# A decoder trunk's first 80 microseconds: loads and copies of the prologue put in another order

## The chip, the cores and the metric

One core of a Trainium2 chip. The time is the device time of one execution in microseconds (us); smaller is better. The profile is of one execution, the times are of several.

## The reference

Two layers (DEPTH = 2) of a decoder trunk for two groups of tokens with the same weights: a prompt of 512 tokens and 8 decode sequences of 4 tokens (32 tokens), width 1024.

```
sh1, sc1, g1, sh2, sc2, g2 = adaln(c, wm, bm)     # silu(c) @ w_mod + b_mod, 6 x 1024 columns
xn = rmsnorm(x, n1) * (1 + sc1) + sh1
a_q, a_kc, ... , m_if = split(xn @ wi, points)    # 2852 columns
x = x + g1 * (concat([a_out, m_out]) @ wo)        # sparse attention beside an mLSTM
xn2 = rmsnorm(x, n2) * (1 + sc2) + sh2
x = x + g2 * conv_ffn(xn2, ...)                   # up, causal conv, silu, gate, down
```

Everything is float32. Only what stands ahead of the first `xn @ wi` is touched here: the loads of x, of the conditions c (one row for the prompt, eight for decode) and of a block of constants, the first four of the twelve column parts of `silu(c) @ w_mod` (sh1 and sc1), and the sums of squares of the first rmsnorm.

## The kernel before, in words

The whole program is written by hand as five instruction streams (SyncE `sp`, TensorE `pe`, ScalarE `act`, VectorE `dve`, GpSimd `pool`), which meet only in semaphores. The tokens are kept turned: `xT` holds, for each of 8 chunks k of 128 features, 544 tokens in the free dimension. Ahead of the layers the prologue does this:

- SyncE issues loads of w_mod, 2 MB each (`load_mod`, L520 to L529): parts 0, 1 and 2 into the three slabs at once, part 3 into slab 1 when part 1 has been used (its turned result counts in `mod_t`). Then it waits for `load_in` (L530) and goes on to layer 0: slab pieces of w_in (`load_in_slab`, L551), each for L = 0 held back at L565 until a count of `mod_t` says that the slab is free; later the pages of the cache.
- GpSimd issues on its own queue the constants (1.6 MB), x_prompt (2 MB), x_sample, c_prompt, c_sample and the page table (L2281 to L2286), all counted in `load_in`, then nine small row loads (`rows_in`, L2294) and three more (L2301).
- ScalarE takes silu of the nine condition rows (L1260). TensorE waits for all six loads and for silu (L645, L646), turns the conditions (L648), then x: for each k four transposes of 128x128 and one of 32x128 (L655, L656) into one of three pairs of PSUM banks.
- For each k ScalarE copies the prompt's part from PSUM to `xT` (L1292), VectorE the decode part (L1618), and ScalarE squares the 544 tokens into one of two buffers `sq` (L1265, in `square`). TensorE adds the squares up over the partitions (`norm_sum`, L629: four calls), one chunk behind the transposes.
- VectorE and ScalarE make 1/rms of it (`inverse_root`, `root`), TensorE spreads it over the partitions (L640, L641) and turns the small rows (L683 to L685). Then for g = 0 to 3 `mod_part` (L669: 32 calls, which the trace shows as 64 matmuls) waits for its weights, ScalarE copies the result out (L1301), `mod_turn` turns it (L678) and VectorE adds the bias (L1667).
- After part 3 ScalarE splits the first w_in piece into a high part (L1308) and GpSimd makes the low part (`low_first`, L2309); VectorE, ScalarE and GpSimd make the scaled and shifted inputs in high and low parts (L1631, L1279, L1638, L2319 to L2323), and TensorE begins the input projection (L778).

Of the kernel before, what the change touches and what calls it, by code (L numbers as in the profile page):

```python
# [14 lines left out]
SEQ = 512  # L15
# [17 lines left out]
KC = D // 128  # L33
TS = NB * NT
TT = SEQ + TS
# [87 lines left out]
_WIDTHS = [a.shape[1] for a in shape_constants()][:len(_NAMES)]  # L123


def trunk_program(nc, A, O):
# [10 lines left out]
    with ctx:  # L137
# [203 lines left out]

        PRO_LOADS = 16 * 6
        pro_silu, pro_ct = ctx.enter_context(nc.semaphore("c_silu")), ctx.enter_context(nc.semaphore("c_transposed"))
        pro_xt = ctx.enter_context(nc.semaphore("x_transposed"))
        pro_copy_p, pro_copy_s = ctx.enter_context(nc.semaphore("x_copied_prompt")), ctx.enter_context(nc.semaphore("x_copied_decode"))
        load_in = ctx.enter_context(nc.semaphore("prologue_loaded"))
        final_tr, final_copy = sig("final_transposed", 10), sig("final_copied", 10)
# [21 lines left out]

        MODS = [(s, 0, c) for s, c in zip((0, 1, 2, 1), range(4))]  # L370
        MOD_FIRST = []
# [5 lines left out]
        MOD_FIRST.append(len(MODS))  # L377
        mod_in = [ctx.enter_context(nc.semaphore(f"mod_weights{s}_loaded")) for s in range(NSLAB)]
        mod_acc, mod_copy, mod_t, mod_add = (sig("mod_accumulated", len(MODS)), sig("mod_part_copied", len(MODS)),
# [132 lines left out]
        def _(sp):  # L512
# [7 lines left out]
            def load_mod(g):  # L520

                s, L, c = MODS[g]
                sp.dma_start(slab[s][:, :].rearrange("p (k n) -> p k n", k=8),
                             wmod[L, :, :, 512 * c:512 * c + 512]).then_inc(mod_in[s], 16)

            for g in range(4):
                if g == 3:
                    sp.wait_ge(mod_t.sem, mod_t.at(2))
                load_mod(g)  # L529
            sp.wait_ge(load_in, PRO_LOADS)  # L530
            flat = lambda a: a.rearrange("l n p a k d -> (l n) p (a k d)")
            cmp_pool, sel_pool = flat(A["cache_cmp_kv"]), flat(A["cache_sel_kv"])

            for L in range(DEPTH):
# [26 lines left out]
                for i in range(4):  # L561
                    if i in (0, 1, 3):
                        load("in", (0, 1, 1, 2)[i], [])
                    if L == 0 and i in (0, 1, 3):
                        sp.wait_ge(mod_t.sem, mod_t.at((1, 4, 4, 3)[i]))  # L565
                    load_in_slab(i)
# [52 lines left out]
        def _(pe):  # L619
# [23 lines left out]
            for s in range(NSLAB):  # L643
                pe.sem_inc(slab_out[s], 1)
            pe.wait_ge(load_in, PRO_LOADS)  # L645
            pe.wait_ge(pro_silu, 1)  # L646
            for k in range(KC):
                ins = tr(ps[7][:, 9 * k:9 * k + 9], crow[0:9, 128 * k:128 * k + 128], idn(9))  # L648
            ins.then_inc(pro_ct, 1)
            for k in range(KC):  # L650
                if k >= 3:
                    pe.wait_ge(pro_copy_p, k - 2)
                    pe.wait_ge(pro_copy_s, k - 2)
                for t in range(PT_):
                    tr(ps[2 * (k % 3)][:, 128 * t:128 * t + 128], xrow[:, t, 128 * k:128 * k + 128], ident)  # L655
                tr(ps[2 * (k % 3) + 1][:, 0:TS], crow2[0:TS, 128 * k:128 * k + 128], idn(TS)).then_inc(pro_xt, 1)  # L656
                if k:
                    norm_sum(0, k - 1)
            norm_sum(0, KC - 1)
            spread(0)  # L660

            def mod_part(g, bank):

                s, _, _ = MODS[g]
                pe.wait_ge(*mod_loads(g))
                wv = slab[s][:, :].rearrange("p (k n) -> p k n", k=8)
                for k in range(KC):
# [11 lines left out]

            pe.wait_ge(pro_copy_p, KC)  # L680
            pe.wait_ge(pro_copy_s, KC)
            pe.wait_ge(rows_in, ROWS)
# [573 lines left out]
        def _(act):  # L1256
            A_ = nc.scalar.activation
            drain = act.drain
            act.wait_ge(load_in, PRO_LOADS)
            A_(crow[0:9, :], crow[0:9, :], ACT.Silu).then_inc(pro_silu, 1)  # L1260
# [29 lines left out]
            for k in range(KC):  # L1290
                act.wait_ge(pro_xt, k + 1)
                A_(xT[:, k, 0:SEQ], ps[2 * (k % 3)][:, :], ACT.Copy).then_inc(pro_copy_p, 1)  # L1292
                act.wait_ge(pro_copy_s, k + 1)
                drain()
                square(0, k)
# [310 lines left out]
        def _(dve):  # L1606
# [9 lines left out]
            for k in range(KC):  # L1616
                dve.wait_ge(pro_xt, k + 1)
                cp(xT[:, k, SEQ:TT], ps[2 * (k % 3) + 1][:, 0:TS]).then_inc(pro_copy_s, 1)  # L1618

# [659 lines left out]
        def _(pool):  # L2279
            ld = pool.dma_start  # L2280
            pool.dma_start(cst[:, :], A["shape_constants"][:, 0:sum(_WIDTHS)]).then_inc(load_in, 16)  # L2281
            ld(xrow[:, :, :], A["x_prompt"][0].rearrange("(t p) d -> p t d", p=128)).then_inc(load_in, 16)
            ld(crow2[0:TS, :], A["x_sample"].rearrange("b t d -> (b t) d")).then_inc(load_in, 16)
            ld(crow[0:1, :], A["c_prompt"]).then_inc(load_in, 16)
            ld(crow[1:9, :], A["c_sample"]).then_inc(load_in, 16)
            ld(pages_sb[:, :], A["page_table"].rearrange("b n -> (b n)").unsqueeze(0)).then_inc(load_in, 16)  # L2286
            r8 = lambda a: a.rearrange("l (k n) -> (l k) n", n=128)
# [179 lines left out]
```

## Time and profile before

| | |
|---|---|
| times of three runs | 1967.26, 1955.88, 1967.9 us (median 1967.26) |
| the profiled execution | 1970.02 us, of it a span of 1968.2 us |
| TensorE busy | 1742.1 us, 89% of the span |
| VectorE, ScalarE, GpSimd busy | 919.3, 617.9, 206.2 us |
| mean granted TensorE clock | 0.919 of full speed |
| DMA | 218.82 MB, mean 111 GB/s |

An engine's busy time says how much work it has; where the time of the whole comes from is read from what TensorE waits for in each stretch.

### The profile page before, as it was taken

Reading aid. Unit: us, or ns where it says so; the run is one execution under the profiler, and the core shown is the slowest. Engines: PE = TensorE matmul, PEld = TensorE weight load, DVE = VectorE, ACT = ScalarE, POOL = GpSimd, SP = SyncE. Lnnn points to the kernel's source line nnn. Section 1 sums busy time; section 2 is a strip of 40 time slices with the busy share of each in tenths; the row PEclk is TensorE's granted clock in tenths of the full one; section 3 lists DMA queues with packets and bytes.
Section 4 is the critical chain, followed back from the end, with each engine's and each line's share of the span. In section 5 each row is a group of like instructions: output and inputs, shape, how many; then the busy total and the mean of one; then the engine's idle time right before and its main releaser. Section 6 shows DMA issues by size and latency. Waiting matters only on the chain.

```text
span 1968.2 us, 37164 instructions
## 1 busy us (share of the span) xinstructions
PE 1742.1 (89%) x14719; PEld 1544.3 (78%) x14719; DVE 919.3 (47%) x2318; ACT 617.9 (31%) x1173; POOL 206.2 (10%) x317
## 2 busy tenths in 40 slices
PE   4699997977879999999979998788768999999996
PEld 3599865545779999999969986534558899999995
DVE  0433434534545555555453343453452645545643
ACT  2232133532324224223232223353231523323313
POOL 2101002432100000000010100133310000000001
PEclk9799978978889999999979998787879999999998
DMA  6435385348522222221123528410772122222201
GB/s 217 132 97 175 87 299 180 111 126 233 106 74 87 86 83 87 85 85 43 46 79 93 182 92 303 122 33 24 220 148 86 44 86 85 85 85 85 85 22 50
DMA packets 154282, 218.82 MB, mean 111 GB/s; under 512 B 11722, under 2 KB 112394, under 8 KB 153964
## 3 DMA queue, kind: packets, MB, share of 16 engines
q1 hardware_dynamic: 145152, 193.23, 31.1%
q0 software_dynamic: 9008, 23.94, 4.4%
q8 instruction: 80, 1.31, 0.3%
q14 instruction: 42, 0.34, 0.1%
HBM read 200.45 MB, written 16.68 MB: 110 GB/s over the span
## 4 chain that ended last, share of the span: by engine, by line
PE 77%; issue 6%; DVE 5%; ACT 3%; DMA 2%; POOL 2%; SPq 2%; DVEq 1%; POOLq 0%; ACTq 0%
PE ps L1177 27%; PE ps L1203 14%; PE ps L778 13%; PE ps L1156 4%; PE ps L868 3%; PE ps L880 2%; PE ps L895 2%; DMA slab<-in_w_up 2%; PE ps L669 2%; PE ps L821 1%; POOL xnT L2371 1%; PE ps L771 1%; PE ps L770 1%; DVE xnT L1631 1%; SPq L538 1%
## 5 line engine op out<-in xcount | busy, mean ns | idle before, releaser
L1177 PE MATMUL ps<-work_r,big_r 128*128 128x272 f32 x1408 | 294.3, 290 | 19.8 <-DVE xnT_r L1656 13.4
L1177 PE MATMUL ps<-work_r,slab_r 128*128 128x272 f32 x1408 | 292.6, 289 | 0.0
L1177 PE MATMUL ps<-xnT_r,big_r 128*128 128x272 f32 x1408 | 290.6, 288 | 0.0
L1177 PEld LDWEIGHTS ps<-work_r,big_r 128*128 128x128 f32 x1408 | 221.4, 189 | 22.8 <-issue 21.5
L778 PE MATMUL ps<-slab_r,work_r 128*128 128x256 f32 (+1 forms) x1024 | 228.6, 287 | 0.0
L1177 PEld LDWEIGHTS ps<-xnT_r,big_r 128*128 128x128 f32 x1408 | 222.8, 189 | 0.0
L1177 PEld LDWEIGHTS ps<-work_r,slab_r 128*128 128x128 f32 x1408 | 221.5, 189 | 0.0
L1656 DVE TENSOR_TENSOR slab_r<-slab,big_r 128x2048 fp32r<-128x2048 f32 (+2 forms) x72 | 168.9, 2349 | 62.0 <-ACT big_r L1536 54.2
L778 PEld LDWEIGHTS ps<-slab_r,work_r 128*128 128x128 f32 x1024 | 174.2, 193 | 2.7 <-issue 2.5
L1203 PE MATMUL ps<-side_r,big_r 128*128 128x272 f32 x704 | 148.3, 292 | 4.9 <-DVE big_r L1656 4.9
L1554 ACT ACTIVATE big<-big,work 128x560 f32<-128x560 f32 x44 | 33.7, 766 | 369.9 <-DVE big L2212 369.9
L1203 PE MATMUL ps<-big_r 128*128 128x272 f32 x704 | 146.2, 289 | 0.0
L1203 PE MATMUL ps<-side_r,slab_r 128*128 128x272 f32 x704 | 145.9, 289 | 0.0
L2160 DVE TENSOR_TENSOR work<-ps,modT 128x32 f32<-128x32 f32 x112 | 21.5, 192 | 254.4 <-PE ps L1203 184.4
L778 PE MATMUL ps<-work_r 128*128 128x256 f32 (+1 forms) x384 | 115.8, 302 | 17.1 <-DVE xnT_r L1638 17.1
L2332 POOL DMA_DIRECT2D out<-work x32 | 18.3, 575 | 1067.2 <-ACT work L1592 822.2
L1203 PEld LDWEIGHTS ps<-side_r,big_r 128*128 128x128 f32 x704 | 111.1, 190 | 7.7 <-DVE big_r L1656 5.4
L1203 PEld LDWEIGHTS ps<-big_r 128*128 128x128 f32 x704 | 111.5, 190 | 0.0
L778 PE MATMUL ps<-work_r,xnT_r 128*128 128x256 f32 (+1 forms) x384 | 111.4, 290 | 0.0
L1203 PEld LDWEIGHTS ps<-side_r,slab_r 128*128 128x128 f32 x704 | 111.1, 190 | 0.0
L1536 ACT ACTIVATE big_r<-slab 128x2048 fp32r<-128x2048 f32 x44 | 84.4, 1918 | 68.4 <-PE ps L1177 55.8
L778 PEld LDWEIGHTS ps<-work_r 128*128 128x128 f32 x384 | 74.8, 195 | 25.3 <-DVE xnT_r L1638 11.5
(432 smaller groups left out, 3129.1 us busy)
## 6 DMA issues: line engine op xcount, KB each, us to landing
slab<-in_w_mod SPq DMA_DIRECT2D x24, 2048.0 KB, 9.2
slab<-in_w_up SPq DMA_DIRECT2D x44, 1024.0 KB, 7.5
slab<-in_w_in SPq DMA_DIRECT2D x20, 1024.0 KB, 5.5
slab<-in_w_down SPq DMA_DIRECT2D x20, 1024.0 KB, 5.8
slab<-in_cache_cmp_kv SPq DMA_DIRECT2D x128, 128.0 KB, 2.0
slab<-in_cache_sel_kv SPq DMA_DIRECT2D x96, 128.0 KB, 2.0
big<-in_cache_win_kv SPq DMA_DIRECT2D x16, 512.0 KB, 5.3
out<-big POOLq DMA_DIRECT2D x16, 448.0 KB
```

The source lines that it names most:

```text
L669: ins = mm(bank[32 * q:32 * q + 32, 0:128], cT[:, k, :], wv[:, k, 128 * q:128 * q + 128], start=k == 0, stop=k == KC - 1, tile_position=(0 ...
L778: ins = mm(ps[n % 4][:, 0:cw], x, fr(wt[:, k, :]), start=k == 0 and m == 0, stop=k == KC - 1 and m == 2)
L868: mm(ps[2 * (s % 2) + k][:, 0:nk], qT[h_, g, 128 * t:128 * t + 128], (ksT, kwT)[br][h_, 0:nk], start=True, stop=True).then_inc(a_s.sem, 1)
L880: ins = tr(ps[4 + k][:, 128 * i:128 * i + 128], Pq[:, u % 4, 128 * i:128 * i + 128], ident)
L895: ins = mm(ps[6][64 * k:64 * k + 64, 128 * i:SEQ], proj[:, i, c + 64 * k:c + 64 * k + 64], PT[:, n % 2, k, 512 * i:384 * i + SEQ], start=b ...
L1156: ins = mm(ps[2 * (c % 3) + b][:, 0:HALF], wt, fr(x[:, k, HALF * b:HALF * b + HALF]), start=k == 0 and n == 0, stop=k == KC - 1 and n == 2)
L1177: ins = mm(ps[2 * half + b][:, 0:HALF], wt, fr(x[:, k, HALF * b:HALF * b + HALF]), start=k == 0 and n == 0, stop=k == KC - 1 and n == 2)
L1203: ins = mm(ps[bank + b][:, 0:HALF], wt, fr(x[:, k, HALF * b:HALF * b + HALF]), start=k == 0 and n == 0, stop=k == n_k - 1 and n == 2)
L1536: A_(fr(hiU[:, q % 2, :, :, :]), src[:, :, :, cc:cc + 128], ACT.Copy).then_inc(w_hi.sem, 1)
L1554: A_(cv[:, s, 0:UPW - 2], cv[:, s, 0:UPW - 2], ACT.Silu, bias=cbias[:, s:s + 1]).then_inc(u_si.sem, 1)
L1656: return tt(fr(dst), dst, fr(hi).bitcast(F), ALU.subtract)
L2160: tt(tmp.rearrange("p (b t) -> p b t", b=NB), hi[:, SEQ - HALF:HALF].rearrange("p (b t) -> p b t", b=NB), bc(gs, 2, NT), ALU.mult)
```

## The change

Five edits, all in the prologue:

1. The constants, x_prompt and x_sample are issued by SyncE on its own queue, ahead of the w_mod parts. They count in semaphores of their own (`k_in`, `x_in`); the conditions and the page table stay on GpSimd's queue and count in `c_in`.
2. w_mod part 3 gets a place of its own, in the unused columns 4096 to 8191 of `big`, so that its load waits for nothing. The pieces of w_in for slab 1 wait for a lower count.
3. TensorE waits for the constants, then silu, turns the conditions, and only then waits for x.
4. VectorE copies both parts of each turned chunk from PSUM to `xT`; ScalarE only squares. One semaphore `pro_copy` takes the place of two, and ScalarE's `drain` is gone.
5. `norm_sum` runs two chunks behind the transposes instead of one.

```diff
-        MODS = [(s, 0, c) for s, c in zip((0, 1, 2, 1), range(4))]
+        MODS = [(s, 0, c) for s, c in zip((0, 1, 2, 3), range(4))]
...
+        mod_at = [t[:, :] for t in slab] + [big[:, 4096:8192]]
...
+            sp.dma_start(cst[:, :], A["shape_constants"][:, 0:sum(_WIDTHS)]).then_inc(k_in, 16)
+            sp.dma_start(xrow[:, :, :], A["x_prompt"][0].rearrange("(t p) d -> p t d", p=128)).then_inc(x_in, 16)
+            sp.dma_start(crow2[0:TS, :], A["x_sample"].rearrange("b t d -> (b t) d")).then_inc(x_in, 16)
             for g in range(4):
-                if g == 3:
-                    sp.wait_ge(mod_t.sem, mod_t.at(2))
                 load_mod(g)
-            sp.wait_ge(load_in, PRO_LOADS)
+            sp.wait_ge(c_in, 48)
...
-                        sp.wait_ge(mod_t.sem, mod_t.at((1, 4, 4, 3)[i]))
+                        sp.wait_ge(mod_t.sem, mod_t.at((1, 2, 2, 3)[i]))
...
-            pe.wait_ge(load_in, PRO_LOADS)
+            pe.wait_ge(k_in, 16)
             pe.wait_ge(pro_silu, 1)
             for k in range(KC):
                 ins = tr(ps[7][:, 9 * k:9 * k + 9], crow[0:9, 128 * k:128 * k + 128], idn(9))
             ins.then_inc(pro_ct, 1)
+            pe.wait_ge(x_in, 32)
             for k in range(KC):
                 if k >= 3:
-                    pe.wait_ge(pro_copy_p, k - 2)
-                    pe.wait_ge(pro_copy_s, k - 2)
+                    pe.wait_ge(pro_copy, k - 2)
...
-                if k:
-                    norm_sum(0, k - 1)
+                if k >= 2:
+                    norm_sum(0, k - 2)
+            norm_sum(0, KC - 2)
             norm_sum(0, KC - 1)
...
-            act.wait_ge(load_in, PRO_LOADS)
+            act.wait_ge(c_in, 48)
...
-                act.wait_ge(pro_xt, k + 1)
-                A_(xT[:, k, 0:SEQ], ps[2 * (k % 3)][:, :], ACT.Copy).then_inc(pro_copy_p, 1)
-                act.wait_ge(pro_copy_s, k + 1)
-                drain()
+                act.wait_ge(pro_copy, k + 1)
                 square(0, k)
...
                 dve.wait_ge(pro_xt, k + 1)
-                cp(xT[:, k, SEQ:TT], ps[2 * (k % 3) + 1][:, 0:TS]).then_inc(pro_copy_s, 1)
+                cp(xT[:, k, 0:SEQ], ps[2 * (k % 3)][:, :])
+                cp(xT[:, k, SEQ:TT], ps[2 * (k % 3) + 1][:, 0:TS]).then_inc(pro_copy, 1)
...
-            pool.dma_start(cst[:, :], A["shape_constants"][:, 0:sum(_WIDTHS)]).then_inc(load_in, 16)
-            ld(xrow[:, :, :], A["x_prompt"][0].rearrange("(t p) d -> p t d", p=128)).then_inc(load_in, 16)
-            ld(crow2[0:TS, :], A["x_sample"].rearrange("b t d -> (b t) d")).then_inc(load_in, 16)
-            ld(crow[0:1, :], A["c_prompt"]).then_inc(load_in, 16)
-            ld(crow[1:9, :], A["c_sample"]).then_inc(load_in, 16)
-            ld(pages_sb[:, :], A["page_table"].rearrange("b n -> (b n)").unsqueeze(0)).then_inc(load_in, 16)
+            ld(crow[0:1, :], A["c_prompt"]).then_inc(c_in, 16)
+            ld(crow[1:9, :], A["c_sample"]).then_inc(c_in, 16)
+            ld(pages_sb[:, :], A["page_table"].rearrange("b n -> (b n)").unsqueeze(0)).then_inc(c_in, 16)
```

## Rows read from the trace of the kernel before

**Rows 1.** Windows: stretch, length, each engine's busy us, granted clock, DMA share, GB/s
```profile
0.00:82.00 82.00, 37.92 (x403) 26.74 (x403) 19.57 (x40) 22.61 (x35) 17.45 (x26) 0.86 0.61 209
82.00:300.00 218.00, 211.99 (x1930) 189.18 (x1929) 79.83 (x196) 58.27 (x124) 17.47 (x23) 0.94 0.48 154
```
**Rows 2.** Timeline of TensorE and ScalarE, 21 to 40 us
```profile
21.12 1.05 ACT L1260 ACTIVATE work<-work 9x1024 f32<-9x1024 f32 x1 [19.08 <-DMA pages_sb<-in_page_table]
...
23.24 1.11 PE L655 MATMUL ps<-shape_constants,work 128*128 128x128 f32 x4
...
26.63 1.12 PE L655 MATMUL ps<-shape_constants,work 128*128 128x128 f32 x4
...
36.13 1.12 PE L655 MATMUL ps<-shape_constants,work 128*128 128x128 f32 x4
...
37.52 0.60 ACT L1292 ACTIVATE xT<-ps 128x512 f32<-128x512 f32 x1 [0.56 <-PE ps L656]
38.20 0.66 ACT L1265 ACTIVATE big<-xT 128x544 f32<-128x544 f32 x1
...
38.91 0.68 PE L629 MATMUL ps<-big,shape_constants 128*32 128x136 f32 x8 [0.81 <-ACT big L1265]
```
**Rows 3.** Timeline, 44 to 72 us: from the first mod part to the input projection
```profile
44.50 3.64 PE L669 MATMUL ps<-slab,cT 128*32 128x128 f32 x64
...
48.80 1.95 PE L669 MATMUL ps<-slab,cT 128*32 128x128 f32 x64
...
52.00 14.31 SPq L558 DMA_DIRECT2D slab<-in_w_in  x5
...
59.69 3.64 PE L669 MATMUL ps<-slab,cT 128*32 128x128 f32 x64 [5.59 <-DMA slab<-in_w_mod]
...
63.57 2.11 ACT L1308 ACTIVATE work_r<-slab 128x2304 fp32r<-128x2304 f32 x1
...
65.77 5.03 POOL L2309 TENSOR_TENSOR slab_r<-slab,work_r 128x2304 fp32r<-128x2304 f32 x1 [54.68 <-ACT work_r L1308]
...
71.50 0.58 PE L778 MATMUL ps<-work_r 128*128 128x288 f32 x1 [7.30 <-DVE xnT_r L1638]
```
**Rows 4.** DMA issues, 0 to 150 us: count, KB each, median us to landing
```profile
slab<-in_w_in SPq DMA_DIRECT2D x5, 1024.0 KB, 5.3
...
work<-in_x_prompt POOLq DMA_DIRECT2D x1, 2048.0 KB, 17.3
...
pages_sb<-in_page_table POOLq DMA_DIRECT2D x1, 0.2 KB, 16.8
```
**Rows 5.** DMA issues, 0.7 to 1.2 us: w_mod part 0
```profile
slab<-in_w_mod SPq DMA_DIRECT2D x1, 2048.0 KB, 14.7
```
**Rows 6.** Windows of the first 35 us: the last column is GB/s moved
```profile
5.00:10.00 5.00, 0.00 (x0) 0.00 (x0) 0.00 (x0) 0.00 (x0) 5.00 (x11) 1.00 1.04 433
10.00:15.00 5.00, 0.00 (x0) 0.00 (x0) 0.00 (x0) 0.00 (x0) 1.08 (x2) 1.00 1.01 395
...
30.00:35.00 5.00, 5.00 (x38) 2.92 (x33) 0.50 (x3) 3.63 (x6) 0.00 (x0) 1.00 0.11 41
```
**Rows 7.** GpSimd's small loads later: DMA issues of 290 to 480 us
```profile
side<-in_state_mlstm_n POOLq DMA_DIRECT2D x2, 8.0 KB, 5.5
```
**Rows 8.** Source line L2417, GpSimd's load of the conv history
```profile
DMA to landing us min/median/max: 11.7/15.0/18.3
```
**Rows 9.** Groups of VectorE copies from PSUM: busy us, mean ns, idle before
```profile
L1992 DVE COPY work<-ps 128x512 f32<-128x512 f32 x24 | 16.6, 691 | 22.3 <-PE ps L991 22.1
...
L1618 DVE COPY xT<-ps 128x32 f32<-128x32 f32 x8 | 1.5, 191 | 12.6 <-PE ps L656 12.6
```
**Rows 10.** Timeline of SyncE's queue: the issue of w_mod part 2
```profile
1.89 10.11 SPq L523 DMA_DIRECT2D slab<-in_w_mod  x1
```
**Rows 11.** Windows from part 3 on: the figure before DMA share is the clock
```profile
60.00:65.00 5.00, 3.80 (x65) 2.84 (x57) 0.58 (x3) 1.61 (x2) 0.00 (x0) 0.50 0.48 132
...
85.00:100.00 15.00, 15.00 (x117) 14.81 (x116) 4.74 (x11) 3.79 (x7) 0.00 (x0) 0.97 0.04 11
```

## Blind prediction of the change's time

> **What bounds the kernel now.** I read the windows first. In the first 82 us TensorE is busy for 37.92 us, and from 82 to 300 us for 211.99 of 218 [rows 1]. The reader is to see two things there: the change lies wholly in a stretch where TensorE mostly waits, and right behind it TensorE is full, so what the prologue saves moves everything behind it forward and nothing behind it takes it back by waiting for a transfer. The gain can't be larger than a part of the 44 us that TensorE doesn't work in these 82. Then I read the timeline, for what ends each wait.
>
> - Until 21 us nothing runs. ScalarE's silu starts at 21.12, released by the load of the page table, the last of the six [rows 2]; that load needed 16.8 us, and x_prompt 17.3 [rows 4], while SyncE's queue carried w_mod parts nobody needed until 44.50 [rows 3]. DMA moved 433 and 395 GB/s from 5 to 15 us [rows 6]: the transfers are not slow, they share, and the needed bytes come with unneeded ones.
> - From 23.24 to the last norm sum, which starts at 38.91, the turned chunks set the pace: one each (36.13 - 26.63) / 5 = 1.90 us [rows 2], with TensorE busy for 5.00 of 5 us from 30 to 35 [rows 6].
> - From 44.50 the four mod parts run. Part 3 starts only at 59.69, after 5.59 us of waiting for its weights [rows 3].
> - From there a fixed chain leads to the projection: ScalarE's split at 63.57, GpSimd's low part at 65.77, TensorE's first product at 71.50 [rows 3].
>
> **Part 1, the load order.** SyncE's queue now carries constants (1630.5 KB), x_prompt (2048 KB) and x_sample (128 KB) first, 3.90 MB. A 1024 KB load alone needs 5.3 us from issue to landing [rows 4]; at 395 GB/s its bytes take 2.65, so 2.65 us are start and completion. That queue begins at about 0.8 us (part 0's issue in the window of [rows 5]), so x is there at 0.8 + 2.65 + 3.90 / 0.395 = 13.3 us. GpSimd's small loads (some 0.46 MB with the 256 KB gains) share the engines; if all come ahead of x they add 1.2 us. I take half: 13.8, and TensorE starts with x at 13.9 in place of 23.24, **9.3 us** earlier. Bounds: 12.5 us (at the 433 GB/s of [rows 6], nothing shared) and 15 us, so 10.7 to 8.2. That SyncE's queue serves its loads one after the other is seen in w_mod part 0: landed 14.7 us after its issue [rows 5], with two more parts behind it and half of the rate going to GpSimd's queue.
>
> This holds only if silu and the turned conditions are ready by 13.9. From the landing of the last condition load to the first transpose of x it was 23.24 - 21.07 = 2.2 us (silu's start at 21.12 less 0.05 of waking [rows 2]), so the cover ends if `c_in` fills later than 11.7. GpSimd issues the three at 1.3 to 2.8 us. The nearest row for a small load on its queue while SyncE's is full is 8 KB in 5.5 us [rows 7], which gives 8.3; the far row is the conv history, 16 rows of 11 KB, with 11.7 to 18.3 us [rows 8], which gives 14 to 21. I take the nearer row, since the three loads are 36 KB together, and keep the other as a rival. The nine small row loads are needed first at about 34 us; even as late as in the far row they are there.
>
> Of the queues passed: GpSimd's sheds three issues, some 2 us that nobody waited for. SyncE's gets three loads ahead of the w_mod parts. One issue there can hold the queue for 10.11 us when two parts are ahead of it [rows 10]; with four parts it may be held until about 30 us, and SyncE's next duty, the first w_in piece, falls due at 39. The weights: the queues ran dry in the slice from 30 us on, in which they moved 41 GB/s [rows 6], so at 30.5; 2.1 MB more are moved now (part 3 comes in the same burst), so part 3 lands at 30.5 + 5.3 + 1 = 37, and part 0 at 13.8 + 5.3 = 19, where it is needed at 34.6. Every part is early.
>
> **Part 2, norm sums two behind and copies on VectorE.** The pace of 1.90 us is TensorE's own work, and its instructions stay the same, so the pace stays. What goes is the wait for the first square: chunk 2 began 3.39 us after chunk 0 [rows 2]; without a sum between them it begins after 2 x 1.28 = 2.56 (1.28 is the pace of 1.90 less 0.62 for a sum, which [rows 2] bound by its 0.68 from first start to last end), and chunk 7 at 4.46 + 4 x 1.90 = 12.06 after chunk 0 in place of 12.89. Against that stands the last chunk's tail, which is serial: VectorE's copy takes 0.69 us [rows 9] where ScalarE's took 0.60 [rows 2], and the decode copy of 0.19 [rows 9] now runs behind it instead of beside it; some of it overlaps, so the tail grows by 0.2 us (0.1 to 0.3). The cover of the copies elsewhere is large: 0.88 us of VectorE and 0.66 of ScalarE in a pace of 1.90. Sum: 0.83 - 0.2 = **0.6 us**, 0.3 to 0.8. With both edits the last sum starts at 13.9 + 15.05 = 29.0 in place of 38.91: 9.9 us.
>
> **Part 3, a place for mod part 3.** Nothing between 38.91 and 44.50 is changed, so part 0 starts at 34.6. Parts follow at 1.95 + 0.66 = 2.61 us (48.80 less the end of part 0 at 48.14, plus the length of part 1) [rows 3], so in the profile of before part 3 could have begun at 48.80 + 2 x 2.61 = 54.02. It began at 59.69: 5.67 us. It also took 3.64 us where part 1 took 1.95 [rows 3]; the granted clock from 60 to 65 us is 0.50, the 1.2 GHz level [rows 11], and TensorE had been idle before it. Directly behind part 2 it runs like part 1: 1.69 us, and 0.15 in its turn. Sum **7.5 us**; if the clock falls or rises otherwise, 5.7 to 7.5. (Part 0 took 3.64 us as well, beside a granted 1.00 in the windows: its duration, not that column, says that it ran at the lower level. It may run so again; if it should find the clock up, 1.7 us more are won, and if part 1 is still at the lower level, 1.7 lost.)
>
> **Part 4, the first w_in piece.** It used to be issued at 52.00 [rows 3]. Its own wait (`mod_t` 1, part 0 turned) was met when part 1 began, at about 48.9, and SyncE hung on part 3's slab. Now it is issued at 48.9 - 9.9 = 39.0 and lands some 6 us later (5.3 for 1024 KB [rows 4], it has 1152), at 45.2. ScalarE wants it at 63.57 - 17.4 = 46.2. So it is just hidden, by 1.0 us; what it comes later than that costs as much again. I take nothing, bound 1 us lost. The other pieces of w_in come 20 us earlier, which is worth nothing: behind 82 us TensorE didn't wait for them [rows 1]. Split, low part, shift and scale (63.57 to 71.50) are untouched and just move.
>
> **Sum.** 9.3 + 0.6 + 7.5 = 17.4 us. The profiled execution of 1970.02 us becomes 1952.6; against the median of 1967.26 that is 1949.9. **Forecast 1950.** The bounds of the terms together give a gain of 13.2 to 20.7 us, or 1946.6 to 1954. A measurement here tells about 1%, 19.7 us, from no change, and the forecast stands just inside it: a real gain that is nearly all of 1%.
>
> **Rival A: the conditions come late (1956).** x is early, but silu waits for three small loads on GpSimd's queue. If they come like the conv history, at 14 to 21 us, take 17.5 [rows 8], TensorE starts x at 19.7, and the first term shrinks from 9.3 to 3.5: gain 11.6, 1955.7. Against it speak [rows 7], and the old order itself: x_prompt, issued at 2.0, landed at 19.3, and the page table, three loads on, at 21.1 [rows 2, 4], 0.6 us for each small one beside a full SyncE queue. For it: the pieces now ahead are long rows (12.7 KB of constants, 4 KB of x), and a small load may have to let whole runs of them pass. The Trainium skill, "DMA: Bandwidth & Descriptors", section "Queues, rings and completion order", says that each DMA engine goes round the queues that have work in whole packets, some 9 to 17 descriptors and up to 64. By that rule a condition load could wait for an engine's share of the constants and the next for one of x, which would put this rival's time in the forecast's place; the trace of before has only short pieces in SyncE's queue and can't show it.
>
> **Rival B: slower, the small loads come last (1974).** The same place, taken to its end: what is on GpSimd's queue lands only when SyncE's has run dry, at about 36.3 us now. Then x starts at 38.5, 15.3 us later than before; less 0.6 and 7.5 that makes 7.2 us lost, 1974.5. It decides from `c_in` at 21.07 + 8.1 = 29.2 us on. Against it: on GpSimd's queue the page table landed at 21.1 us, 9 us before SyncE's, just as full, ran dry [rows 2, 6].
>
> **Rival C: the gain is there at 82 us and the clock moves the rest (1943 or 1957).** The three runs of before lie 12 us apart with the same program, more than most terms here, and the clock falls and rises at places that depend on when TensorE pauses: after the mod parts it stood at 0.50, and only from 85 us on at 0.97 [rows 11]. The new pause, between part 3 and the first product, is about 8 us, as the old second one was, so I expect the same fall. If the clock should stay up, 1.6 us are won at the start of the projection, and later phases may turn out either way by some 6 us.
>
> **How the numbers follow.** The forecast's mechanism 0.70; A 0.14; B 0.03; C 0.13. With the spread of the runs (12 us between three) laid over the forecast, about four in ten of its share, and half of C's, end beyond 19.7 us: 0.35 faster by over 1%. Slower by over 1% needs B and more: 0.02. The rest, 0.63, is within 1%. Range 1940 to 1960: above it takes in A and a forecast that falls on a slow run, below a forecast that falls on a run like the 1955.88.
>
> **What would show it.** Right: the page (or the conditions) releases silu before 10 us; the first transpose of x waits for x_prompt and starts at 13 to 15; the last norm sum is 15.0 to 15.2 us behind it; the fourth mod part starts 0.7 us behind the third and takes 1.95 us; GpSimd's low part starts at 47 to 50; the first product at 52.5 to 56, 16 to 19 us earlier than 71.50; from there the same work in the same time. Wrong: silu released after 11.7 (A) or 29 us (B); a wait of ScalarE for the w_in piece; a fourth mod part of 3.64 us; a stretch behind the prologue that is longer by more than a microsecond or two at another granted clock (C).

## The result, and the profile after

The changed kernel takes 1949.28 us (median of 13 runs, 1945.96 to 1956.36), the kernel before 1961.3 us (13 runs, 1950.9 to 1967.9). The ratio is 0.9946 with an interval of 0.9926 to 0.9966: faster by 10.6 us, 6.7 to 14.5, clearly different from nothing and within 1%. The forecast said 1950, by a gain of 17.4 us against a median of three runs that lay 6 us too high; the time was met, the gain was three fifths of what was forecast. Three single executions further down (of 2009, 2042 and 2832 us, one in each of three versions) ran at a granted clock of 0.56 to 0.83 where the others have 0.92, and count in no ratio.

The timeline of the changed kernel from the load of the conditions to the first input product, against [rows 2, 3]:

```profile
8.27 1.06 ACT L1262 ACTIVATE work<-work 9x1024 f32<-9x1024 f32 x1 [6.23 <-DMA pages_sb<-in_page_table]
...
17.52 1.12 PE L657 MATMUL ps<-shape_constants,work 128*128 128x128 f32 x4 [7.05 <-DMA work<-in_x_sample]
...
32.52 0.68 PE L631 MATMUL ps<-big,shape_constants 128*32 128x136 f32 x8 [0.50 <-ACT big L1267]
...
38.10 2.78 PE L672 MATMUL ps<-slab,cT 128*32 128x128 f32 x64
...
41.72 7.03 SPq L560 DMA_DIRECT2D slab<-in_w_in  x5
...
46.77 1.96 PE L672 MATMUL ps<-big,cT 128*32 128x128 f32 x64
...
48.97 2.11 ACT L1307 ACTIVATE work_r<-slab 128x2304 fp32r<-128x2304 f32 x1
...
51.16 5.03 POOL L2306 TENSOR_TENSOR slab_r<-slab,work_r 128x2304 fp32r<-128x2304 f32 x1 [41.90 <-ACT work_r L1307]
...
56.90 0.58 PE L780 MATMUL ps<-work_r 128*128 128x288 f32 x1 [7.45 <-DVE xnT_r L1638]
```

Read it as a chain of differences. Silu starts 12.9 us earlier, but x's first transpose only 5.7 (17.52 for 23.24), and TensorE waited 7.05 us for it: silu is no longer what is late, x is. The last norm sum is 6.4 us earlier, part 0 too, part 3 12.9 us (46.77 for 59.69), the first product **14.6 us** (56.90 for 71.50). The loads in the first 60 us of that trace, against [rows 4], with the columns as there:

```profile
work<-in_x_prompt SPq DMA_DIRECT2D x1, 2048.0 KB, 14.6
...
shape_constants<-in_shape_constants SPq DMA_DIRECT2D x1, 1630.5 KB, 6.9
...
work<-in_x_sample SPq DMA_DIRECT2D x1, 128.0 KB, 15.8
...
pages_sb<-in_page_table POOLq DMA_DIRECT2D x1, 0.2 KB, 5.8
```

and its windows, the last column GB/s, against [rows 6]:

```profile
5.00:10.00 5.00, 0.53 (x5) 0.56 (x6) 0.00 (x0) 1.06 (x1) 4.26 (x8) 1.00 1.00 351
10.00:15.00 5.00, 0.47 (x5) 0.37 (x4) 0.23 (x1) 0.00 (x0) 0.00 (x0) 1.00 0.98 296
```

The DMA engines are as busy as before (shares 1.00 and 0.98) and move 351 and 296 GB/s where they moved 433 and 395. The constants are in at 7.7 us, x_prompt at 15.8, x_sample, 128 KB behind it, only at 17.5.

In all the two profiled executions are 24 us apart (1970.02 and 1945.99), which is 9 more than the prologue gives. The profiled run of before was slower than all 13 timed ones. With the matmuls of the two traces matched one by one, the lead of the changed kernel is 14.6 us at the first product, 15.2 at 300 us of the kernel before, 11.8 at 330, 7.3 at 600, 9.6 at 1060, 6.1 at 1200 and 22.4 at 1600. So it loses 3.4 us from 300 to 330 and 4.5 more up to 600, and what it wins late is mostly a wait that one execution of before had in layer 1. Both are taken up below.

### The profile page after: what moved, and what is told of

It is laid out like the page before. It is cut to its first block, busy times and chain, and to the rows that moved or that the text cites. A ratio compares the mean times of both kernels' runs of the same rounds, so it can differ in the third digit from the quotient of the medians.

```text
span 1944.2 us, 37157 instructions
## 1 busy us (share of the span) xinstructions
PE 1733.2 (89%) x14719; PEld 1540.3 (79%) x14719; DVE 924.1 (48%) x2326; ACT 613.2 (32%) x1165; POOL 203.6 (10%) x314
## 4 chain that ended last, share of the span: by engine, by line
PE 78%; issue 5%; DVE 5%; ACT 3%; DMA 2%; POOL 2%; SPq 2%; DVEq 1%; POOLq 0%; ACTq 0%
PE ps L1179 27%; PE ps L1205 14%; PE ps L780 13%; PE ps L1158 4%; PE ps L870 2%; PE ps L897 2%; PE ps L882 2%; PE ps L672 2%; DMA slab<-in_w_up 2%; POOL xnT L2368 1%; PE ps L823 1%; PE ps L773 1%; PE ps L772 1%; SPq L540 1%; DVE xnT L1631 1%
## 5 line engine op out<-in xcount | busy, mean ns | idle before, releaser
L1179 PE MATMUL ps<-work_r,big_r 128*128 128x272 f32 x1408 | 295.0, 291 | 19.3 <-DVE xnT_r L1656 13.4
```

The lines of the kernel that those rows point to most:

```text
L1179: ins = mm(ps[2 * half + b][:, 0:HALF], wt, fr(x[:, k, HALF * b:HALF * b + HALF]), start=k == 0 and n == 0, stop=k == KC - 1 and n == 2)
```

## The experiments

In each, "x" is the start of the first transpose of x, "product" that of the first input product. Before: 23.24 and 71.50; changed: 17.52 and 56.90. These two come from one trace each; the unchanged parts of other traces show how far such a time repeats (the first run of the pair without state stores has the prologue of before, product at 71.27; the second that of the changed kernel, 57.33).

**Each part alone.**

The order alone:

```diff
...
+            sp.dma_start(cst[:, :], ...).then_inc(k_in, 16)      # then x_prompt, x_sample: x_in
             for g in range(4):
                 if g == 3:
                     sp.wait_ge(mod_t.sem, mod_t.at(2))
                 load_mod(g)
-            pe.wait_ge(load_in, PRO_LOADS)
+            pe.wait_ge(k_in, 16)
...
+            pe.wait_ge(x_in, 32)                                  # ahead of x's transposes
```

> The kernel before with the load order alone (constants, x_prompt, x_sample first on SyncE's queue, conditions and pages on GpSimd's); mod part 3 still waits for slab 1, copies and sums as before. Theory: the order alone makes x's first transpose start at 17.5 us as in the changed kernel (before: 23.24), 5.7 us earlier, and the whole chain up to the first input product moves by that: 71.5 - 5.7 = 65.8 us. Rival 1: the late landing of x comes from part 3 being in the same burst: then x starts here at 14 to 15 us. Rival 2: the wait for part 3's weights eats the gain (its load is issued by a fixed event, not earlier): first product at 71.

x at 17.36, product at 61.92, 1949.75 us in one run (before on that chip 1966.03). x came as the theory had it, so part 3 in the burst is not what makes x late. The product came 3.9 us earlier than expected. The timeline shows why:

```profile
20.75 1.12 PE L660 MATMUL ps<-shape_constants,work 128*128 128x128 f32 x4
...
24.26 0.66 PE L660 MATMUL ps<-shape_constants,work 128*128 128x128 f32 x4
...
30.63 0.68 PE L633 MATMUL ps<-big,shape_constants 128*32 128x136 f32 x8 [0.96 <-ACT big L1270]
...
36.22 2.51 PE L674 MATMUL ps<-slab,cT 128*32 128x128 f32 x64
...
50.12 3.64 PE L674 MATMUL ps<-slab,cT 128*32 128x128 f32 x64 [5.43 <-DMA slab<-in_w_mod]
```

Four transposes took 1.12 us at 20.75 and 0.66 at 24.26: by their duration the clock came up to its upper level in the middle of them (the granted clock reads 1.00 there, and in the kernel before too), which it did in neither the kernel before nor the changed one. From x to the last sum it was 13.3 us in place of 15.7, and part 0 took 2.51 for 3.64. 2.4 + 1.1 us of this gain are that, 5.9 the order, 0.2 a shorter wait for part 3, which was still 5.43 us.

Part 3's own place alone:

```diff
-        MODS = [(s, 0, c) for s, c in zip((0, 1, 2, 1), range(4))]
+        MODS = [(s, 0, c) for s, c in zip((0, 1, 2, 3), range(4))]
...
-                if g == 3:
-                    sp.wait_ge(mod_t.sem, mod_t.at(2))
...
```

> The kernel before with a place of its own for mod part 3 alone. Theory: x starts at 23.2 us as before, the fourth part starts 0.7 us behind the third and runs in 1.95 us, first input product at 71.5 - 7.5 = 64.0 us. Rival: four parts in the burst delay GpSimd's loads of constants and x, which share the engines: x at 25 us or later, product at 66 us or later.

x at 23.4, product at 61.92 (9.6 us earlier), 1949.13 us in one run. The rival falls: four parts in the burst delay GpSimd's loads by nothing that shows. Part 3 ran at 51.80 for 1.96 us, right behind part 2. Here too the clock came up in the transposes (part 0 at 42.76 for 44.50, and 3.16 us long): 2.2 of the 9.6 us. The place gives 7.4.

Copies and sums alone:

```diff
-                if k:
-                    norm_sum(0, k - 1)
+                if k >= 2:
+                    norm_sum(0, k - 2)
+            norm_sum(0, KC - 2)
             norm_sum(0, KC - 1)
...
-                A_(xT[:, k, 0:SEQ], ps[2 * (k % 3)][:, :], ACT.Copy).then_inc(pro_copy_p, 1)
+                cp(xT[:, k, 0:SEQ], ps[2 * (k % 3)][:, :])        # on VectorE
```

> The kernel before with the copies on VectorE and the sums two chunks behind alone. Theory: from the first transpose of x to the last norm sum 15.0 us in place of 15.67, first input product at 71.5 - 0.6 = 70.9 us, with part 3's wait moved by as much. Rival: VectorE's longer copies and ScalarE's wait for them take the gain back: 15.7 us, product at 71.5 us.

The last sum at 38.36, 15.00 us behind x for 15.67 and 0.55 us earlier than 38.91 (x came at 23.36); the product at 69.83, 1.7 us earlier, of which 0.7 are a part 0 of 2.91 us and 0.4 part 3's load, which needed a little less. 1958.32 us in one run. The term was right in the prologue, and this trace has something else, which comes below.

All but the order:

> The kernel before with part 3's own place, the copies on VectorE and the sums two behind, but the old load order. Theory: the parts add up: x starts at 23.2 us, first input product at 71.5 - 7.5 - 0.6 = 63.4 us (up to 2.5 less if the clock rises earlier), run time 6 to 10 us below the kernel before. On where the rest of the changed kernel's gain went: in three of three traces with the new load order and with the state stores, TensorE waited 5 to 7 us ahead of the second norm of layer 0 for a late w_up, in none of the three traces with the old order. If that belongs to the order, this kernel doesn't show it in layer 0 and its runs are no slower than those of the changed kernel by more than 3 us; if it is chance, it may show it and its runs are some 6 us slower than the changed kernel's. In the same way a stretch of layer 0 (303 to 342 us) took 3.4 us longer in the four traces with the copies' edit and in no other: if it belongs to the edit, it is here.

x at 23.16, product at 62.22 (expected 63.4, up to 2.5 less; part 0 took 2.47). 1955.78 us, ratio 0.9976 (0.9955 to 0.9997): 5 us faster, 1 to 9. The parts add up in the prologue. With the order on top the ratio is 0.9946 (0.9926 to 0.9966): the two intervals overlap, so that the order adds to the run time what it adds in the prologue (5.9 us by the ratios) is likely, but barely clear of nothing. Of the two readings that the expectation offered neither fits whole: TensorE waited only 1.7 us in layer 0, as if the lateness belonged to the order, and the runs are some 6 us slower than the changed kernel's, as if it were chance. The stretch of layer 0 took 40.8 us, halfway between the two lengths.

**What makes x late.** Four versions of the changed kernel. The three edits below make one version each; the fourth has the first and the third:

```diff
+            pool.wait_ge(x_in, 32)       # rows and gains later: here
             r8 = lambda a: a.rearrange("l (k n) -> (l k) n", n=128)
...
```

```diff
+            pool.wait_ge(x_in, 32)       # the gains alone later: here
             load_gains(0)
```

```diff
             sp.dma_start(crow2[0:TS, :], ...).then_inc(x_in, 16)
+            sp.wait_ge(x_in, 32)         # weights after x
             for g in range(4):
                 load_mod(g)
```

Rows and gains later:

> The changed kernel with GpSimd waiting for x before it issues its nine row loads and three loads of gains (0.42 MB). Theory (the small loads of GpSimd's queue slow x): x starts at 13.9 to 14.5 us in place of 17.52, and the first input product comes at 53 to 54 us in place of 56.9. Rival (the engines fall out of step by themselves, with the w_mod parts behind x in the same queue filling them): x starts at 16.5 to 17.5 us.

The gains alone later:

> The changed kernel with only the three gain loads (260 KB of the 0.46 MB) held back until x is there. Theory: DMA moved only 141 GB/s in a stretch at 13.5 to 15 us, where a 256-byte packet of the b_if gains took 862 ns on each of 16 engines; that stall and the 256 KB are most of the delay, x starts at 14.5 to 15.5 us. Rival: the nine row loads with their short rows are the delay, and x starts at 16 to 17.5 us.

The weights after x:

> The changed kernel with SyncE waiting for x before it issues the four w_mod parts; GpSimd's small loads as in the changed kernel. Theory (GpSimd's small loads slow x, not the w_mod parts behind it in the same queue): x starts at 16 to 17.5 us as in the changed kernel. Rival (DMA engines that are through with x go on with w_mod and take bandwidth from those that aren't): x starts at 14 to 15 us. The mod parts then land at about 17 + 2.6 + 21 = 40 us, part 0 at 25 us, before they are needed at 38 and 46 us.

Rows, gains and weights, all after x:

> The changed kernel with both: GpSimd's row and gain loads and SyncE's w_mod parts held back until x is there. Theory: with nothing beside or behind them the constants and x move at the full rate, x starts at 13.2 to 13.8 us against 14.0 with the small loads alone held back, and the first input product comes at 53.3 to 54 us; the mod parts land by 38 us and part 0 by 21 us, before they are needed. Run time 14 to 18 us below the kernel before. Rival: the gap between the end of x and the first w_mod bytes delays part 3 or the first w_in piece, and ScalarE's split starts later than 46 us.

| held back until x is there | x | product |
|---|---|---|
| nothing (changed kernel) | 17.52 | 56.90 |
| w_mod | 15.52 | 55.08 |
| gains | 15.22 | 54.69 |
| rows and gains | 13.93, 14.2 | 54.06, 53.46 |
| rows, gains, w_mod | 13.66 | 53.24 |

The timeline of the version with rows and gains later, and under it that with all three:

```profile
13.93 1.11 PE L657 MATMUL ps<-shape_constants,work 128*128 128x128 f32 x4 [3.74 <-DMA work<-in_x_sample]
```

```profile
13.66 1.12 PE L658 MATMUL ps<-shape_constants,work 128*128 128x128 f32 x4 [3.38 <-DMA work<-in_x_sample]
```

With GpSimd's twelve small loads out of the way x starts at 13.93 and 14.2. So 3.3 to 3.6 us of lateness go with 0.42 MB of small loads, for which their bytes account for 1.1 at 395 GB/s. But the loads are only half of it: w_mod held back with the small loads left in place gives 2.0 us too (15.52, between what theory and rival said), and once the small loads are gone w_mod costs just 0.3 to 0.5. Both rivals were partly right: the two work together. What fits all five rows is that the small loads put the DMA engines out of step, and an engine that is through with x goes on to w_mod while another still has x to move; no row here shows single engines, so this is argued, not shown. The gains' 260 KB cost 2.3 us, the rows' 160 KB 1.0 to 1.3. The slow packets named in the expectation go with the delay that small loads and w_mod make together: in the three traces that have the order with nothing held back, 15 or 16 packets of 256 bytes took 0.5 to 1.3 us each at about 13.5 us; with gains or w_mod held back none took over 0.03 us before x was there. From 13.5 to 14.0 us DMA moved 36 GB/s in the changed kernel, 180 with the gains held back and 285 with w_mod held back. Whether these packets cause the delay or share its cause is not shown.

The three single runs and the timed version that belong to this: 1944.09 (gains), 1947.99 (w_mod), 1958.84 (rows and gains); all three held back 1951.95 us, ratio 0.9943 (0.9920 to 0.9965). That is 11 us below the kernel before where 14 to 18 were expected, and no better than the changed kernel's 0.9946, though its product comes 3.7 us earlier. The version with rows and gains later was timed:

> The changed kernel with GpSimd's row and gain loads held back until x is there, timed. Theory: the prologue is 17.4 us shorter than before (first input product at 54.1 us, as in its trace), so the runs are about 3 us below the changed kernel's and 14 us (0.7%) below the kernel before's. Rival: the rows that come later make no difference in the run time, or the late w_up in both layers (5 to 6 us each in its first trace) belongs to the new order and costs what was won: 8 to 11 us below the kernel before.

1946.74 us, ratio 0.9914 (0.9885 to 0.9943): 16.8 us faster than before, 11 to 22, for an expected 14. The holding back of w_mod on top makes the prologue 0.2 to 0.8 us shorter and shows no gain in the runs.

**Where the rest went: the copies' edit again.** Rows and gains later, and the copies and sums as in the kernel before:

```diff
-                    pe.wait_ge(pro_copy, k - 2)
+                    pe.wait_ge(pro_copy_p, k - 2)
+                    pe.wait_ge(pro_copy_s, k - 2)
...
-                cp(xT[:, k, 0:SEQ], ps[2 * (k % 3)][:, :])
+                A_(xT[:, k, 0:SEQ], ps[2 * (k % 3)][:, :], ACT.Copy).then_inc(pro_copy_p, 1)   # on ScalarE
```

> The changed kernel with GpSimd's row and gain loads held back until x is there, and with the copies and sums as in the kernel before (ScalarE copies, sums one behind). Theory: x starts at 14.0 us, from there to the last norm sum 15.7 us in place of 15.0, first input product at 54.1 + 0.6 = 54.7 us. The stretch of layer 0 that took 39.1 us in the four traces without the copies' edit and 42.5 in the seven with it (partly so in one more) tells whether that edit causes it: 39.1 here if it does, and then the runs are 2 to 3 us below those of the version with the edit. Rival: that stretch depends on when the work starts against the clock's steps, and takes 42.5 us here too. The late w_up of layer 0 (5 of 6 traces with the new order and the state stores): about 5 us of waiting if it belongs to the order.

x at 14.2, product at 54.30. **1942.05 us, ratio 0.9879 (0.9849 to 0.9910)**: 23.7 us faster than before, 17.7 to 29.6, and the lowest ratio of all. The version that differs from it by the copies' edit alone is the one above, on another chip, with 0.9914: 0.35% or 7 us more, but the intervals overlap, so these two don't show by themselves that the edit costs time. On the same chip the one with the edit, w_mod held back too and a product 1.1 us earlier gave 1951.95 and 0.9943, and there the intervals don't touch; those 12.6 us are far more than the 3.2 that follow, and the rest isn't explained. The traces show the 3.2. The chain in time, in the stretch named (columns: start, us, what); first before, then the changed kernel, then the copies' edit alone, then this version:

```profile
314.99 4.24 PE ps L844 x24
319.23 0.79 PE ps L848 x8
320.02 1.03 PE ps L850 x8
...
322.17 4.72 PE ps L858 x32
```

```profile
300.02 5.38 PE ps L846 x24
305.41 1.18 PE ps L850 x8
306.59 1.03 PE ps L852 x8
...
308.74 6.35 PE ps L860 x32
```

```profile
312.98 5.38 PE ps L843 x24
318.36 1.17 PE ps L847 x8
...
321.68 6.36 PE ps L857 x32
```

```profile
297.21 4.24 PE ps L847 x24
301.45 0.79 PE ps L851 x8
...
304.39 4.71 PE ps L861 x32
```

The same instructions on the same data, 200 us behind the edit: 10.8 us in the first and the last, 13.9 in the two between. They are transposes, behind 8.5 us in which TensorE does one short transpose, and they start at the lower clock; in the one kind the clock comes up during the first 24, in the other one step later. The windows that hold them say so, granted clock 0.76 before and 0.63 after:

```profile
315.00:328.00 13.00, 11.87 (x80) 11.30 (x80) 4.09 (x10) 3.08 (x4) 1.78 (x3) 0.76 0.80 293
```

```profile
300.00:313.00 13.00, 11.85 (x64) 11.59 (x64) 3.15 (x7) 3.07 (x4) 1.76 (x3) 0.63 0.84 304
```

Of the traces with the edit 8 of 9 have the long form, of those without it none of 5 (the ninth is the one with the old order and part 3's place). When the work starts doesn't decide it: the start moved by 17 us between them in either group.

What links a copy at 20 us to the clock at 315 stands in the traces, on ScalarE. In the chain ahead of the transposes it squares eight 128x128 blocks, one after the other. In all nine traces with the edit, and in none of the five without, it stands idle for 0.34 us ahead of one of them, always the same instruction of its stream, and waits there for nothing that the profile shows ("issue"); TensorE's wait behind it is 4.19 us for 3.92. The changed kernel, and then TensorE's short transpose before and after:

```profile
290.52 0.31 ACT L1380 ACTIVATE work<-big 128x128 f32<-128x128 f32 x1 [0.34 <-issue]
```

```profile
310.37 0.30 PE L678 MATMUL ps<-shape_constants,aTs 128*128 128x128 f32 x1 [3.92 <-DVE modT L1667]
```

```profile
295.40 0.30 PE L681 MATMUL ps<-shape_constants,aTs 128*128 128x128 f32 x1 [4.19 <-DVE modT L1667]
```

The transposes so start 0.27 us later, counted from the last work of TensorE. In the five traces of the short form without the edit they start 3.9 us after the granted clock has fallen, and it rises 2.9 us after their start; in the eight of the long form they start 4.1 to 4.4 us after the fall, and it rises 5.8 to 6.1 us after their start. Before (fall at 311.08, start at 314.99), then after (fall at 295.86, start at 300.02), the clock being the figure before the DMA share:

```profile
311.10:317.80 6.70, 2.81 (x13) 2.81 (x14) 4.48 (x5) 0.60 (x1) 1.78 (x3) 0.50 0.83 246
318.00:324.70 6.70, 5.57 (x51) 5.31 (x49) 2.39 (x5) 2.33 (x3) 0.00 (x0) 1.00 1.04 378
```

```profile
295.90:306.00 10.10, 5.97 (x29) 5.98 (x29) 5.96 (x7) 2.58 (x4) 1.76 (x3) 0.50 0.93 273
306.20:309.40 3.20, 2.07 (x18) 1.81 (x18) 1.01 (x3) 0.29 (x1) 0.00 (x0) 1.00 1.05 380
```

In the ninth trace with the edit the pause is there, but the clock fell 6.7 us ahead of the transposes and rose 3.5 us behind their start: the short form. So the rival had a point too: in these traces the form goes with where the start stands between the clock's steps, and the edit moves it by 0.27 us. No run sets that pause by itself, so this last link is not shown by an experiment but read from 14 traces that agree, and why ScalarE pauses at that instruction is open. Not every such difference goes with the edit: from 1060 to 1200 us a stretch is 3.2 to 3.5 us longer in six of the nine traces with it and in two of the five without.

**Where the rest went: the late w_up.** In the profiled run of before TensorE waited 11.4 us ahead of the second norm of layer 1 (the waits of TensorE from 1440 to 1500 us), in the changed kernel 6.7 us at the same place of layer 0 (485 to 545 us). Before, then after:

```profile
PE ps L629 <- ACT big L1265: 11.4, 1, 11.4
```

```profile
PE ps L631 <- ACT big L1267: 6.7, 1, 6.7
```

The chain behind both leads to a 1 MB load of w_up, which landed a median of 34.6 us and 30.9 us after its issue, where the same load of layer 0 in the kernel before took 24.9. It shares the engines with GpSimd's stores of the decode groups' mLSTM states. So those were left out of both kernels:

```diff
...
                 for s_ in range(2):
                     for q_ in range(2):
                         pool.wait_ge(ms_Cc.sem, ms_Cc.at(3 * q_ + 3, L))
                         h = 2 * q_ + s_
-                        put(s_C[L][:, h].rearrange("b k v -> k b v"), ...)
-                        pool.dma_start(s_n[L][:, h].rearrange("b k -> k b"), ...)
```

> The kernel before without the stores of the decode groups' mLSTM states C and n (16 DMAs in two layers; those two outputs are left out). In the trace of before the load of w_up ahead of the second norm of layer 1 lands only 37.7 us after its issue, beside those stores, whose packets take up to 1 us each, and TensorE waits 11.4 us; in layer 0 1.2 us. Theory: without the stores w_up lands in time in both layers, the run time falls by 5 to 15 us and the spread of the runs shrinks from 17 us to under 6 us. Rival: the late landing has another cause (the load of the conv history, the order of the queue): no change in time and spread.

1952.24 us, ratio 0.9945 (0.9926 to 0.9963) against before, and runs from 1946.9 to 1956.9 where before has 1952.9 to 1970.3: 10.8 us faster with a spread of 10 us for 17. The DMA issues of that stretch of layer 0:

```profile
slab<-in_w_up SPq DMA_DIRECT2D x2, 1024.0 KB, 19.8
...
work<-in_state_ffn_conv POOLq DMA_DIRECT2D x1, 176.0 KB, 3.8
```

w_up lands after 19.8 us for 24.9, and the conv history, which needed 11.7 to 18.3 us [rows 8], after 3.8. The theory holds in its main point; the spread shrank less than it said.

> The changed kernel without the same stores (those two outputs are left out). Theory: the prologue's gain is 14.6 to 15.0 us in every run, and what hides part of it in the medians is the chance landing of w_up; with that taken away this kernel is 13 to 16 us faster than the kernel before without the stores. Rival: the moved start gives back some 4 us later in the kernel for a reason of its own: the two differ by 8 to 12 us here too.

1945.54 us, ratio 0.9911 (0.9884 to 0.9938) against before. By the ratios it is 0.34%, 6.7 us, below the same without the stores in the kernel before, and the two intervals allow 0 to 13. Expected were 13 to 16; the rival said 8 to 12 and lies inside those bounds. The theory that only chance hides the 14.6 us doesn't hold: of its missing part the copies' edit explains 3.2 us (this trace has the long form too), and some 4 us by the medians stay open.

Whether the late w_up belongs to the new order is not settled. In layer 0 TensorE waited 5.2 to 11.1 us in seven of eight traces with the order and the stores, and 1.1 to 1.7 in four of four with the old order. Yet the trace with 11.1 is of the best version, whose profiled run, 1950.2 us, was the slowest of its six, and that of before, with its 11.4 in layer 1, slower than its 13. A profile shows one draw; the runs say that the lateness comes and goes in both kernels.

## Why the forecast was right, and where it was off

- **Part 1, the load order: the term mis-sized.** Forecast 9.3 us, measured 5.7. The step that failed is "if all come ahead of x they add 1.2 us. I take half": small loads were charged by half of their bytes at the full rate, 0.6 us. They cost 3.3 to 3.6: 1.9 by themselves (15.52 for 13.66) and the rest only with w_mod behind x, for which the forecast has no term. The base under it, 2.65 us and 3.90 MB at 395 GB/s, gives a start at 13.4 with no small load in the way; held back they leave 13.9 to 14.2, and 13.66 with w_mod held back too, so it was right to within 0.3 to 0.8 us. The bound of 15 us was too near as well.
- The cover of silu held: the page table needed 5.8 us, for the 5.5 of [rows 7], and silu started at 8.27. Rival A is dead, and with it what the forecast made of the Trainium skill, "DMA: Bandwidth & Descriptors", section "Queues, rings and completion order": the small loads didn't wait for an engine's whole share of the constants or of x: the three landed 5.8 to 5.9 us after their issue each, at 7.2 to 8.3 us, where the constants were in at 7.7 and x_prompt at 15.8. The other direction of the same sharing was the one that cost, small loads holding up large ones. Rival B is dead with it.
- **Part 2: right in the prologue.** 15.00 us from x to the last sum, forecast 15.05; 0.67 us gained, forecast 0.6. Not seen was that this edit would cost 3.2 us at 315 us. "So the pace stays" was also an assumption about the clock: with the clock up, chunks follow faster, as the order alone showed.
- **Part 3: right.** Part 3 followed part 2 and took 1.96 us; the place alone gave 7.4 for 7.5. In the changed kernel 0.9 us came on top, from a part 0 of 2.78 us, a case that the forecast had named.
- **Part 4: right.** The first w_in piece was issued at 41.7 and landed 5.4 us later, 1.9 us before ScalarE could take it.
- **The sum.** 5.7 + 0.7 + 8.2 = 14.6 us in the prologue for 17.4. Of these the runs keep 10.6 (6.7 to 14.5); the 3.2 us of rival C's kind, the clock moving the rest, are about as large as the difference of the two middle values, whose bounds are wide. That rival was named, with 6 us either way, but as chance; it goes with an edit. The statement "nothing behind it takes it back by waiting for a transfer" was read from rows that end at 300 us; in the trace of the changed kernel TensorE waits 6.7 us for a load at 500 us, where it waited 1.2 in that of before.
- That the time came out at 1949.28 for 1950 is luck: the median it stood on was 6.0 us too high (1967.26 from three runs, 1961.3 from thirteen), and the gain was forecast 6.8 us too large. From the median of thirteen the same gain would have given 1943.9.

## What to carry to other kernels

Small loads that nobody needs yet are not free because they are small: behind a wait for the data that is urgent, they gave back 3.3 to 3.6 us of x's landing here, three times what their bytes come to, 1.9 of it by themselves and the rest only because 8 MB of weights stood behind x. An edit whose gain is well under a microsecond can cost several elsewhere: here a pause of 0.34 us on ScalarE goes with transposes that run 3.2 us longer because the clock comes up later, so the same stretch should be compared in the traces with and without the edit. And a single profile is a poor witness for a kernel whose loads land by chance: here the median of three runs stood 6 us from that of thirteen.

## What the runs showed that was not expected

- TensorE's clock came up during the transposes and norm sums in two of 14 traces (four transposes in 0.66 us, 1.12 before), and not in those of the kernel before and after; a prologue's length differs by up to 2.4 us by that alone.
- 176 KB into 16 partitions needed 11.7 to 18.3 us beside stores of a strided state and 3.8 us without them; the stores delayed 1 MB loads by 5 us and cost the kernel before 10.8 us in all (7.3 to 14.5).
